# Latent attention: one stacked tile of 128 rows per head for the scores, and the bias transfer cut in four pieces

## The reference, cut to what matters

```python
def mla_attention(q_nope, q_pe, k_nope, k_pe, v, pos):
    scale = (MLA_NOPE + MLA_ROPE) ** -0.5          # 64 + 32
    ...
    logits = (jnp.einsum('bqhd,bkhd->bhqk', qn, k_nope)
              + jnp.einsum('bqhr,bkr->bhqk', qp, k_pe))
    logits = logits.astype(jnp.float32) * scale
    mask = key_chunk[None, :] <= (qpos // CHUNK)[:, None]
    p = jax.nn.softmax(jnp.where(mask[None, None], logits, -jnp.inf), axis=-1)
    return jnp.einsum('bhqk,bkhd->bqhd', p, v)
...
bias = rel_bias[t5_bucket(idx - qpos[None, :, None])]   # dsa_attention, added to its logits
```

## Time and profile before

| what | value |
|---|---|
| three runs | 1469.69, 1471.28 (median), 1473.66 us |
| the profiled execution | 1471.64 us, its span 1469.8 us |
| PE, PEld, DVE, ACT, POOL busy | 99%, 78%, 63%, 31%, 57% of the span |
| chain of work that ended last, by engine | PE 89%, DVE 6%, issue 1%, ACT 1%, PEld 1% |
| granted TensorE clock | mean 0.998 of full speed |
| latent attention loop | from 1126.1 to 1247 us |

### The profile page before, as it was taken

One profiled execution on the slowest core, in us unless ns is written; L12 is line 12 of the kernel. 1 busy time (PEld: TensorE's weight loads), 2 busy tenths in 40 slices (PEclk: granted clock), 3 DMA queues, 4 the chain that ended last, 5 costly groups with the idle time before them and its releaser, 6 DMA issues.

```text
span 1469.8 us, 20093 instructions
## 1 busy us (share of the span) xinstructions
PE 1451.5 (99%) x7044; PEld 1150.7 (78%) x7044; DVE 931.6 (63%) x1685; ACT 450.3 (31%) x887; POOL 833.7 (57%) x675
## 2 busy tenths in 40 slices
PE   9999999999999999999999999999999999999998
PEld 7888777766888898788888888887767777767887
DVE  6768896777248334577776773325777777685245
ACT  4456432376122122321010010112333344464112
POOL 5634333534666787467767777776655254444662
PEclk9999999999999999999999999999999999999999
DMA  5221211211333333132333333334324531323332
GB/s 198 87 58 44 58 41 46 72 58 58 115 100 96 113 108 113 59 100 86 100 101 93 96 99 101 114 101 130 95 86 137 94 101 58 115 72 113 103 97 76
DMA packets 37018, 135.60 MB, mean 92 GB/s; under 512 B 4297, under 2 KB 4553, under 8 KB 36297
## 3 DMA queue, kind: packets, MB, share of 16 engines
q1 hardware_dynamic: 33264, 121.13, 27.5%
q10 hardware_dynamic: 3672, 13.35, 3.5%
HBM read 127.64 MB, written 6.82 MB: 91 GB/s over the span
## 4 chain that ended last, share of the span: by engine, by line
PE 89%; DVE 6%; issue 1%; ACT 1%; PEld 1%; DMA 0%; PEldq 0%; DVEq 0%; ACTq 0%
PE pair L626 25%; PE pair L628 24%; PE pair L627 24%; PE pair L911 4%; PE pair L939 3%; PE pair L923 2%; PE pair L800 1%; PE pair L787 1%; PE pair L835 1%; DVE dx L2106 1%; DVE selm L2382 0%; DVE dx L2103 0%; PE pair L746 0%; PE pair L745 0%; PE pair L822 0%
## 5 line engine op out<-in xcount | busy, mean ns | idle before, releaser
L581 POOL TENSOR_TENSOR wL<-ring,wH 128x1024 fp32r<-128x1024 f32 x223 | 548.0, 2457 | 18.6
L626 PE MATMUL pair<-nH,wH 128*128 128x512 f32 x1064 | 426.5, 401 | 2.1 <-DVE nL L1761 0.8
L628 PE MATMUL pair<-nH,wL 128*128 128x512 f32 x1064 | 414.9, 390 | 0.0
L627 PE MATMUL pair<-nL,wH 128*128 128x512 f32 x1064 | 414.8, 390 | 0.0
L578 POOL TENSOR_TENSOR tick<-tick 128x1 f32<-128x1 f32 x223 | 58.1, 260 | 593.8 <-PE pair L628 548.1
L626 PEld LDWEIGHTS pair<-nH,wH 128*128 128x128 f32 x1064 | 199.7, 188 | 62.7 <-issue 18.9
L579 POOL TENSOR_SCALAR wH<-ring 128x1024 fp32r<-128x1024 f32 x223 | 236.5, 1061 | 0.0
L628 PEld LDWEIGHTS pair<-nH,wL 128*128 128x128 f32 x1064 | 199.7, 188 | 42.7
L627 PEld LDWEIGHTS pair<-nL,wH 128*128 128x128 f32 x1064 | 199.9, 188 | 41.1 <-issue 1.9
L1604 ACT ACTIVATE sgb<-cv 128x512 f32<-128x512 f32 x22 | 13.9, 634 | 209.5 <-DVE cv L2291 209.5
L626 PE MATMUL pair<-aH,wH 128*128 128x512 f32 x176 | 68.5, 389 | 0.0
(11 more groups left out here) (403 smaller groups left out, 2659.4 us busy)
## 6 DMA issues: line engine op xcount, KB each, us to landing
ring<-stream SPq DMA_DIRECT2D x223, 512.0 KB, 3.5
gvec<-gv ACTq DMA_DIRECT2D x1, 2560.0 KB
hT<-xT SPq DMA_DIRECT2D x4, 512.0 KB, 5.9
x_d<-hT ACTq DMA_DIRECT2D x1, 2048.0 KB, 7.3
toep<-gvec ACTq DMA_DIRECT2D x8, 256.0 KB, 3.3
hT<-x_d ACTq DMA_DIRECT2D x1, 2048.0 KB, 8.6
out<-yo SPq DMA_DIRECT2D x4, 512.0 KB, 3.6
cD<-const_d ACTq DMA_DIRECT2D x1, 1345.0 KB, 6.4
```

The costliest lines, as they stand in the source:

```text
L581: pool.tensor_tensor(low, ring[:, r, :], high.bitcast(F32), ALU.subtract).then_inc(split_done, 1)
L626: mm(out, a[0], b[0], start=first, stop=False)
L627: mm(out, a[0], b[1], start=False, stop=False)
L628: return mm(out, a[1], b[0], start=False, stop=last)
```

## The change

Every head gets one tile of 128 rows for its query and one for its key: 64 rows (`own_rows`) hold its own part, in the half where the product leaves it; the other 64 (`shared_rows`) hold the rotary part. One product of 128 rows then makes the scores of a head; `kpz` and its semaphore go. The copies to `qn` and `kn` become two copies of 64 rows each, eight copies on ACT move the rotated `qp` into the stacked tiles, and DVE writes the masked rotary key eight times on 64 rows. The bias DMA becomes four of two heads each, issued in steps 1, 3, 5 and 7.

```diff
--- before.py
+++ after.py
@@ -433,12 +433,15 @@
         ckL = place("ckL", [P, 2, S], F32R)
         kv_scale = place("kv_scale", [P, S])
         qi = place("qi", [P, 2, S], at=d0 + 4 * (4 + 2 + 4 + 2 + 4 + 4 + 6) * S)
+        qp = place("qp", [P, 2, S])
         assert top[0] <= d0
         top[0] = d0
-        qn = place("qn", [P, 4, S])
-        qp = place("qp", [P, 2, S])
-        kn = place("kn", [P, 4, S])
-        kpz = place("kpz", [P, 2, S])
+        qs4 = place("qs4", [P, 4, S])
+        qs2 = place("qs2", [P, 2, S])
+        ks4 = place("ks4", [P, 4, S])
+        ks2 = place("ks2", [P, 2, S])
+        qs_last = place("qs_last", [P, 2, S], at=sums0)
+        ks_last = place("ks_last", [P, 2, S], at=rl0)
         vA = place("vA", [P, ST, S])
         za = place("za", [P, 4, S])
         b0 = top[0]
@@ -476,6 +479,18 @@
         def tile_factors(b):
 
             return E[:, b, :, :].rearrange("p (d two) s -> p d (two s)", d=2)[:, :, :2 * LQ]
+
+        def stacked(x, h):
+
+
+            parts_of = (qs4, qs2, qs_last) if x == "q" else (ks4, ks2, ks_last)
+            return parts_of[0][:, h, :] if h < 4 else parts_of[h // 2 - 1][:, h % 2, :]
+
+        def own_rows(h):
+            return slice(64 * (h % 2), 64 * (h % 2) + 64)
+
+        def shared_rows(h):
+            return slice(64 - 64 * (h % 2), P - 64 * (h % 2))
 
         def vcol(name, c):
             i = VEC[name] + c
@@ -523,7 +538,7 @@
         f_made, lf_made, lf_turned, lh_made, lft_made, zero_one = (
             sem(n) for n in ("f_made", "lf_made", "lf_turned", "lh_made", "lft_made", "zero_one"))
         dec_done, exp_done, x_made, k_made = (sem(n) for n in ("dec_done", "exp_done", "x_made", "k_made"))
-        rep_done, rep_out, kpz_made = sem("rep_done"), sem("rep_out"), sem("kpz_made")
+        rep_done, rep_out = sem("rep_done"), sem("rep_out")
         sc_done, masked, s_made = sem("sc_done"), sem("masked"), sem("s_made")
         cross_done, cross_out, o_done, o_out = (sem(n) for n in ("cross_done", "cross_out", "o_done", "o_out"))
         o_sq, o_sum, o_std, o_diag, o_wide = (sem(n) for n in ("o_sq", "o_sum", "o_std", "o_diag", "o_wide"))
@@ -1207,10 +1222,7 @@
             barrier()
 
             def mla_terms(h, i, keys):
-                qs = slice(P * i, P * i + P)
-                rows = head_rows(h)
-                return [(qn[rows, h // 2, qs], kn[rows, h // 2, keys]),
-                        (qp[rows, h // 4, qs], kpz[rows, h // 2 % 2, keys])]
+                return [(stacked("q", h)[:, P * i:P * i + P], stacked("k", h)[:, keys])]
 
             attention("mla", mla_terms, lambda h, t, bk: (vA[:, t, 64 * h:64 * h + 64], head_rows(h)), dx, dPT,
                       dsa_beside, lambda n: dsa_product(*DSA_ITEMS[18 + n]))
@@ -1664,16 +1676,29 @@
             index_relu(1)
             sigmoids("z_a", [3])
             index_relu(2)
+            def heads_out(stage, x, c):
+                b, free = product(stage, c)
+                for h in (2 * c, 2 * c + 1):
+                    last = A(stacked(x, h)[own_rows(h), :], b[own_rows(h), :], ACT.Copy)
+                last.then_inc(free, 1)
+
             for s in range(3):
                 for c in (2 * s, 2 * s + 1):
-                    copy_out("uq", c, qn[:, c, :] if c < 4 else qp[:, c - 4, :])
+                    if c < 4:
+                        heads_out("uq", "q", c)
+                    else:
+                        copy_out("uq", c, qp[:, c - 4, :])
                 index_relu(3 + s)
             act.wait_ge(x1_made, DC)
             act.dma_start(x1_d, hT[:, :, :]).then_inc(st_x1, 16)
             for c in range(4):
-                copy_out("ukv_k", c, kn[:, c, :])
+                heads_out("ukv_k", "k", c)
             for i in range(ST):
                 copy_out("ukv_v", i, vA[:, i, :])
+            for h in range(8):
+                if h % 4 == 0:
+                    act.wait_ge(rotated, ROTATE["second"] + 2 + h // 4)
+                A(stacked("q", h)[shared_rows(h), :], qp[own_rows(h), h // 4, :], ACT.Copy)
             barrier()
             def dsa_copy(stage, j):
                 if stage in ("q_b", "k_b"):
@@ -1688,16 +1713,16 @@
             act.wait_ge(st_x1, 16)
 
             def mla_beside(s):
-                if s == 1:
+                if s % 2 and s < 8:
                     act.wait_ge(gv_out, 2)
-                    act.dma_start(gvec, gv[:, None, :].broadcast_to([8, P, TOEP])).then_inc(st_gvec, 16)
+                    act.dma_start(gvec[s - 1:s + 1], gv[s - 1:s + 1, None, :].broadcast_to([2, P, TOEP])).then_inc(st_gvec, 16)
                 for item in dsa_done(s):
                     dsa_copy(*item)
 
             attention("mla", dx, dPT, yaH, beside=mla_beside,
                       tail=lambda n: dsa_copy(*DSA_ITEMS[18 + n]))
             barrier()
-            act.wait_ge(st_gvec, 16)
+            act.wait_ge(st_gvec, 16 * 4)
 
             def load_bias(h, done):
                 act.dma_start(toep[:, h % 4, :], bass.AP(gvec.tensor, h * P * TOEP + P - 1, [[TOEP - 1, P], [1, S]])).then_inc(done, 16)
@@ -2357,8 +2382,9 @@
             dve.wait_ge(rep_out, 3)
             rotate("second", 0, kp[:, :], c_d("cos", 0, S), c_d("sin", 0, S), to=6)
             dve.wait_ge(rotated, ROTATE["second"] + 1)
-            for g in range(2):
-                V.tensor_scalar(kpz[:, g, :], kp[:, :], c_d("parity", g, g + 1), None, ALU.mult).then_inc(kpz_made, 1)
+            for h in range(8):
+                g, rows = h // 2 % 2, shared_rows(h)
+                V.tensor_scalar(stacked("k", h)[rows, :], kp[rows, :], c_d("parity", g, g + 1)[rows, :], None, ALU.mult)
             silu("z_a", [1], za)
             at = {1: 0, 2: 2 * P, 3: 5 * P}
 
```

## The result

The changed kernel takes 1487.56 us (median of 4 runs, 1487.40 to 1487.99) against 1471.42 before: a ratio of 1.0104, 95% interval 1.0088 to 1.0119, so 16 us slower. The forecast was 1466.3, range 1463.8 to 1474. The profiled execution took 1487.43 us, its span is 1485.6 us.

What follows compares the result with a forecast made beforehand. PE was taken to bound the latent attention loop; -6.0 (scores) + 0.3 (key copies) + 0.8 (DVE at the loop's end) = -4.9 us from 1471.64 gave 1466.7, or 1466.3 us as the median of runs; range 1463.8 to 1474.

Steps and rivals of the forecast that it cites:

- the bias transfer: ACT's bias DMA in the loop: four quarters take 1.29 us to issue in all, the end comes in time, cost nothing.
- Rival (B): Bias transfer: two engines at 0.38 us a packet end at 1330, 83 us late, about 1549 us; chance 0.09.
- The scores: PE's score products in the attention loop: 0.40 us saved in 12 steps, 0.30 in 4, 6.0 us less.
- The joints' explanation: PE's scores: array halves already work side by side, so stacking removes only four fixed joints of about 0.1 us per step.
- The key copies: ACT's copies for the key ahead of the loop: a second copy of 0.61 us makes PE wait 0.3 us more.
- The eight query copies: ACT's rotary copies ahead of the loop: 4.9 us of work fits in its 10.3 us barrier wait, cost nothing.
- DVE at the loop's end: DVE's last normalisation meets PE's transposes without slack, so PE waits and 0.8 us are given back, bounds 0 and 1.2.
- The transfer's pace: Bias transfer in the loop: two engines per piece, one piece after another, half the present rate, ending about 1239.5.
- (A): Bias transfer slowed by weight loads on its two engines ends at 1259.5, 12 us late; typically 1469 us; chance 0.22.
- The stream: Weight loads and POOL's splits in the loop: PE, arriving earlier, waits for none; cost nothing, bound 2.9 us.

Runs made afterwards that it cites:

- spaced pieces: The changed kernel with its four two-row bias pieces issued at steps 1, 3, 7 and 11 instead of 1, 3, 5 and 7: 1466.06 us, ratio 0.9961.
- the two halves: The changed kernel with two bias transfers of four rows each, at steps 1 and 5, in place of the four pieces: 1477.89 us.
- stacking alone: The changed kernel with its stacked tiles, but the bias transfer in one piece at step 1 as before the change: 1469.34 us, ratio 0.9987.

## Why the prediction was wrong

**The step that failed** is one sentence on the bias transfer: "Issuing it takes ACT 1.29 us; four quarters should take the same in all." They took 1.25, 0.62, 13.73 and 20.19 us; the first quarter alone cost as much as the whole. I had costed the transfer's pace in detail and asked only who waits for its end. The instruction that starts it is itself work of ACT, in ACT's order. I took its length from a queue that was empty, while my own forecast had up to two and a half pieces queued on two engines. Behind it stood the copies of line 1301 and 1481, on which PE depends within the same step. Rival (B) saw a danger next to it, two engines too slow, but put its price at the loop's end, where it never came.

**The price.** Against the spaced pieces, where nothing else differs, the span is 1485.6 - 1464.3 = 21.3 us longer. PE is busy 1448.6 instead of 1445.8 us, 2.8 more, about what 3.5 and 3 us at half the clock behind the two idle times cost; the other 18.5 are idle time, 17.8 of it in the two waits shown. That it is the block, and not the pieces or the two engines as such, is shown by the runs with pieces further apart: the same packets on the same two engines until 1242.1, and 1466.06 us.

**The scores:** right. 0.40 us in step 1. With neither block nor late loads (spaced pieces), PE comes to the transposes at 1232.33 instead of 1237.86, 5.5 us earlier, though its first scores start 0.2 later (1126.33 for 1126.12): 5.7 us from the 16 steps, forecast 6.0. 5.5 us is also what the span gains (1469.8 to 1464.3); the forecast was 4.9 net. **The joints' explanation:** right too. "The halves of the array evidently work side by side already" is what the starts show in either order. Within the scores the pairs follow each other in 0.21 us, as single products of 128 rows do (0.215). The 0.40 us lie where half-array and whole-array work meet: 0.32 for 0.23 ahead of the first pair, 0.32 for 0.21 behind it, 0.31 for 0.21 behind the last, and 0.34 for 0.23 for the product after.

**The key copies:** right. PE waits once, at 1105.25, where the changed kernel's timeline has:
```profile
1105.25 0.50 PE L641 MATMUL pair<-ckH,wH 128*128 128x512 f32 x1 [0.19 <-ACT ks L1682]
```
The start before it is 0.57 us earlier instead of 0.23, so 0.3 us lost. **The eight query copies:** right, nothing; ACT's wait at the barrier went from 10.3 to 5.2 us. **DVE at the loop's end:** the lag came as forecast, and nothing was given back. What DVE starts at 1222.17 it starts 4.8 us earlier in the kernel with spaced pieces (1217.40), while PE comes 5.5 earlier. One instruction further on makes up for it. The timelines of POOL and DVE, before and with spaced pieces:

```profile
1233.27 2.42 POOL L581 TENSOR_TENSOR wL<-ring,wH 128x1024 fp32r<-128x1024 f32 x1
1234.47 1.50 DVE L2371 TENSOR_SCALAR selm<-selm 128x512 f32<-128x512 f32 x1
```
```profile
1227.73 2.40 POOL L596 TENSOR_TENSOR wL<-ring,wH 128x1024 fp32r<-128x1024 f32 x1
1229.70 0.72 DVE L2398 TENSOR_SCALAR selm<-selm 128x512 f32<-128x512 f32 x1
```

It ends 0.28 us behind POOL's split before and 0.29 with spaced pieces (0.28 to 0.29 in 13 of the 14 kernels), and takes 0.43 us in the two halves, where no split runs beside it. So it stands until the split is done. POOL follows PE, its split came 5.5 us earlier, and the 0.8 us fell out of DVE's wait for POOL. The forecast had not looked there. Nor did DVE and PE "meet with no slack": the second head's transposes, which need the last normalisation, start at 1238.29, 0.4 us behind its end. That the spaced pieces came so near the forecast's number is in part luck: the scores gave 0.3 us less, and DVE cost 0.8 less.

**The transfer's pace:** right, two engines, 1241.9 for 1239.5; rivals (A) and (B) had 1259.5 and 1330. The rules that I had weighed, engines by the slowest dimension and one way out for four neighbouring partitions (the Trainium skill, "DMA: Bandwidth & Descriptors", section "Why a DMA increments its semaphore by 16 and not by 1", and "SBUF — State Buffer", section "Door 1: The DMA port swizzle"), both hold here: 1.9, 8.3 and 11.8 engines busy on average for two, eight and one row (the last transfer has 128 copies as its slowest dimension); and 0.38 us a packet from partitions 0 to 7 against 0.11 from partitions four apart, with the same eight engines. They gave the right end of the transfer and nothing on the cost of its start.

**The stream:** 0, as taken. In the kernel as changed the block hides it, but in the one with spaced pieces POOL waited 7.7 us for loads and PE never for a split. The bound of 2.9 us is what the transfer cost where it stayed whole (stacking alone, span 1467.2 against 1464.3). The two halves paid more, 8.0 us of PE's waits. So what the loads lose depends on how slow the packets beside them are and on how long they run.

## What to carry to other kernels

A DMA instruction is work of the engine that issues it: before splitting one, work out how much will still lie on the DMA engines that carry it when the next is issued, and what the issuing engine owes others behind the instruction. Split along the dimension that doesn't choose the engines (here columns, not rows), or give the source rows partitions four apart. And a long issue is harmless where nobody waits for the issuing engine: look for the wait, not for the length.

## What the runs showed of the hardware

A DMA instruction on ACT's queue that blocked returned when earlier transfers had 71 to 81 packets of 2560 bytes left on each of their 2, 4 or 8 engines; with one row on 16 engines already at about 10. SP's DMA instructions, 0.33 us each, went out meanwhile. The same 2.6 MB left in 16 us from partitions four apart and in 52 from neighbours. PE ran at 1.2 GHz for 3 to 3.5 us behind idle times of 6 and 12 us. Products of 64 rows on the two halves of the array started 0.01 us apart, in either order of the program. The last `selm` TENSOR_SCALAR of DVE in the loop took 0.43 us alone and 0.71 to 1.50 us beside a split of POOL, and ended 0.28 to 0.29 us behind it.
